# The low part of the late U blocks made by GpSimd between its row gathers instead of by VectorE

## The reference

```python
    def block(xb):
        q = (xb @ w_query).reshape(PEER_BLOCK, PEER_HEADS, 2, PEER_HALF)
        s = jnp.einsum('bhpd,phnd->bhpn', q, sub_keys).astype(jnp.float32)
        top_s, top_i = lax.top_k(s, PEER_TOPK)
        ...
        eid = e1 * PEER_NKEYS + e2
        gate = jax.nn.softmax(best_s, axis=-1)
        u_sel = expert_u[eid]
        act = jax.nn.gelu(jnp.einsum('bd,bhkd->bhk', xb, u_sel).astype(jnp.float32), approximate=False)
        v_sel = expert_v[eid]
        return jnp.einsum('bhk,bhkd->bd', (gate * act).astype(xb.dtype), v_sel)
```

## Time and profile before

| what | value |
|---|---|
| median of 3 runs | 3494.87 us (3494.62 to 3495.22) |
| profiled execution: span from the first to the last instruction | 3500.7 us |
| profiled execution: a time of its own beside the span | none is given |
| mean granted TensorE clock | 0.982 of full speed |

### The profile page before, as it was taken

One profiled execution on the slowest core, in us unless ns is written; L12 is line 12 of the kernel. 1 busy time (PEld: TensorE's weight loads), 2 busy tenths in 40 slices (PEclk: granted clock), 3 DMA queues, 4 the chain that ended last, 5 costly groups with the idle time before them and its releaser, 6 DMA issues.

```text
span 3500.7 us, 56614 instructions
## 1 busy us (share of the span) xinstructions
PE 3350.9 (96%) x21384; PEld 3291.5 (94%) x21384; DVE 2591.7 (74%) x4995; ACT 1018.7 (29%) x1349; POOL 977.2 (28%) x773
## 2 busy tenths in 40 slices
PE   6999999999998999998998899999999999999996
PEld 6999999899998999998997899999999999999996
DVE  5554444233343379999997899999999999999996
ACT  5742222321322232222543122222222222222222
POOL 0000000000000111111002555555555555555550
PEclk8999999999999999999999999999999999999998
DMA  2111011111322232334889999899998999999992
GB/s 105 40 45 36 29 36 64 68 48 42 141 85 73 89 107 102 106 112 136 266 266 307 333 337 328 318 327 326 338 329 317 327 327 340 328 321 321 329 326 104
DMA packets 304353, 698.46 MB, mean 200 GB/s; under 512 B 23873, under 2 KB 124225, under 8 KB 303201
## 3 DMA queue, kind: packets, MB, share of 16 engines
q0 software_dynamic: 98592, 362.97, 28.5%
q1 hardware_dynamic: 104112, 276.89, 23.3%
q10 hardware_dynamic: 101520, 56.89, 5.3%
HBM read 604.44 MB, written 92.22 MB: 199 GB/s over the span
## 4 chain that ended last, share of the span: by engine, by line
PE 77%; DVE 17%; DMA 2%; DVEq 2%; ACT 1%; issue 1%; ACTq 0%; SPq 0%; PEldq 0%
PE PS L1532 29%; PE PS L365 16%; PE PS L1515 14%; PE PS L1223 6%; PE PS L1253 5%; DVE HOTG L2052 3%; PE PS L1447 3%; PE PS L380 1%; DVE HOT L2048 1%; DVE HOT L2049 1%; DVE fold L1980 1%; DVE besti L1924 1%; DVE sc L1915 1%; DVE besti L1916 1%; DVEq L1978 1%
## 5 line engine op out<-in xcount | busy, mean ns | idle before, releaser
L1532 PE MATMUL PS<-AH,VH 128*128 128x368 f32 x2048 | 513.8, 332 | 20.4 <-DVE VL L2075 10.9
L1532 PE MATMUL PS<-AH,VL 128*128 128x368 f32 x2048 | 515.2, 332 | 0.0
L1532 PE MATMUL PS<-AL,VH 128*128 128x368 f32 x2048 | 509.7, 330 | 0.0
L746 POOL DMA_INDIRECT SLOT<-rows_u,EID x256 | 346.4, 1353 | 578.5 <-DVE XLF L2091 257.5
L746 POOL DMA_INDIRECT SLOT<-rows_v,EID x256 | 333.7, 1304 | 205.7 <-DVE SLOT L2082 167.5
L1532 PEld LDWEIGHTS PS<-AH,VH 128*128 128x128 f32 x2048 | 365.2, 189 | 22.7 <-DVE VL L2075 12.1
L1532 PEld LDWEIGHTS PS<-AL,VH 128*128 128x128 f32 x2048 | 366.2, 189 | 0.0
L1532 PEld LDWEIGHTS PS<-AH,VL 128*128 128x128 f32 x2048 | 365.8, 189 | 0.0
L2091 DVE SCALAR_TENSOR_TENSOR XLF<-SLOT,GA,XLF 128x1024 f32<-128x1024 f32 x256 | 328.0, 1281 | 0.5 <-DMA SLOT<-rows_v,EID 0.2
L1109 ACT ACTIVATE VH<-VRAW 128x512 fp32r<-128x512 f32 x256 | 157.8, 628 | 567.7 <-PE PS L1532 567.7
L2082 DVE SCALAR_TENSOR_TENSOR SLOT<-SLOT,XHF 128x1024 f32<-128x1024 f32 x256 | 312.6, 1221 | 3.3 <-DMA SLOT<-rows_u,EID 3.3
(11 more groups left out here) (331 smaller groups left out, 6478.3 us busy)
## 6 DMA issues: line engine op xcount, KB each, us to landing
RAW<-experts_u SPq DMA_DIRECT2D x128, 512.0 KB, 6.4
VRAW<-experts_v SPq DMA_DIRECT2D x256, 256.0 KB, 5.8
gate_matrices<-stg ACTq DMA_DIRECT2D x21, 2048.0 KB, 10.2
GW<-gate_matrices SPq DMA_DIRECT2D x96, 384.0 KB, 7.2
RAW<-weights SPq DMA_DIRECT2D x69, 512.0 KB, 3.6
activations<-AS SPq DMA_DIRECT2D x64, 368.0 KB, 2.4
AS<-activations SPq DMA_DIRECT2D x64, 368.0 KB, 3.0
GW<-gate_matrices SPq DMA_DIRECT2D x32, 320.0 KB, 6.0
```

The source lines that it names most:

```text
L746: pool.indirect_dma_start(out=SLOT[n % NSLOT][:, :], out_offset=None, in_=table, in_offset=bass.IndirectOffsetOnAxis(ap=ids, axis=0)).then ...
L1532: mm = pe.matmul(PS[:, 4 + 2 * (d % 2) + t, 0:CH], w[:, d % 2, c * P:c * P + P], x[:, c, t * CH:t * CH + CH], start=(c == 0 and n == 0), s ...
```

## The change

GpSimd's `u_low(m, slot)` computes the same subtraction as VectorE's did. It stands in the GpSimd program in each group behind the gather pair j = 2, so behind the gather for k = 5 and ahead of that for k = 6 (block m = 2g + 3), and behind the pair j = 5, so behind k = 11 and ahead of k = 12 (block m = 2g + 4). It waits for `u_hi` of its block, and for `u_lo` of the block before. VectorE's two `u_low` of each group are gone; the two of the start (`u_low(1, 0)` and `u_low(2, 1)`) stay with VectorE.

```diff
@@ gpsimd
+            def u_low(m, slot):
+
+                pool.wait_ge(u_lo, m - 1)
+                pool.wait_ge(u_hi, m)
+                pool.tensor_tensor(WL[:, slot, :], RAW[:, slot, :], WH[:, slot, :].bitcast(F32), ALU.subtract).then_inc(u_lo, 1)
+
             for g in range(NG - 1):
                 for j in range(SPR):
                     gather(SPR + 2 * SPR * g + 2 * j, v_rows, g, j)
                     gather(SPR + 2 * SPR * g + 2 * j + 1, u_rows, g + 1, j)
+                    if j == 2:
+                        u_low(2 * g + 3, 0)
+                    if j == 5:
+                        u_low(2 * g + 4, 1)
@@ vector, group_dve
                     dve.tensor_tensor(AL[:, k, :], AF[:, k, :], AH[:, k, :].bitcast(F32), ALU.subtract).then_inc(a_lo, 1)
                     if h == 0:
                         between(1)
-                    if not last:
-                        u_low(2 * g + (3 + h), h)
                     between(2 if h == 0 else SPR if first else 1)
```

## The result

The changed kernel takes 3678.84 us (median of 4 runs, 3672.48 to 3686.21) against 3495.05 us for the kernel before (median of 4 runs), a ratio of 1.0528 (95% interval 1.051 to 1.0545): 183.8 us slower. The profiled execution, the slowest of the four, took 3686.21 us with a span of 3684.5 us, 183.8 us more than the span before.

What follows compares the result with a forecast made beforehand. TensorE was taken to set the time in the steady state. 29 groups x (3.8 us pause + 1.9 us clock) + 3 us for groups 0 and 1 = 168 us more, giving 3660 us, range 3565 to 3725.

Steps and rivals of the forecast that it cites:

- No gain from the work taken off: VectorE, from group 2 on: two subtractions of 1.22 us fewer per group, beside a TensorE that never pauses, worth 0.
- The wait ahead of k = 6 and the chain behind it: GpSimd's queue waits for ScalarE's split; gather for k = 6 starts 6.7 us later, delaying k = 6 to 8, AF and AL.
- The size of the pause: TensorE at pair (0,3), waiting for AL of late block 1: 3.8 us in each group, bounds 2.4 to 5.1 us.
- The subtraction's time: GpSimd's subtraction in the chain: 2.40 us, the median of the selection stage, where the longest was 3.12 us.
- The 4.5 us that stood beside the rule: Pause at pair (0,3) if contention with VectorE made each subtraction take the trace's longest time: 3.8 + 0.7 = 4.5 us.
- The clock: TensorE's lower granted clock behind each pause at pair (0,3): 1.9 us more per group, bounds 0 and 2.9 us.
- The lower bound of 1.1 us: Clock cost read in the 5 us from 1920, behind the 4.08 us pause; 1.9 lies near the middle of 1.1 and 2.9.
- pause without the clock: Rival: gathers land in 5.0 us each, pause at pair (0,3) is 2.4 us and the clock holds: 3565 us, chance 0.24.
- The second subtraction: Gather for k = 12 lands by about 2526, VectorE wants it at about 2526.6: it just fits, counted as 0.
- Groups 0 and 1: Start of the stage, where the full chain doesn't apply: +3 us for both, between -2.3 and +5.4.
- Hidden or faster: Two rivals: gathers land in time, within 3 us of no change, chance 0.04; shorter start pauses give 3488 us, chance 0.03.
- More than one pause in a group: Rival: k = 12 or VL of d = 2 also late, or the long subtraction holds: 3730 us and above, chance 0.09.

Runs made afterwards that it cites:

- e2: Only the second subtraction of a group (behind the gather for k = 11) moved to GpSimd, from group 1 on, against the kernel before: 3495.94 us, ratio 1.0002.
- e10: Both subtractions on GpSimd from group 1 on, behind the gathers for k = 9 and k = 11, against the kernel before: 3509.50 us, ratio 1.0042.
- e4: The kernel before, subtractions left with VectorE, but GpSimd waits for the two splits ahead of the gathers for k = 6 and k = 12: 3573.77 us, ratio 1.0224.
- e5: The changed kernel with VectorE doing AF and AL of late block 1 before rows k = 6, 7 and 8, groups 1 to 31: 3545.04 us, 1.0148 of kernel before.
- e3: The changed kernel with both GpSimd subtractions moved behind the gathers for k = 9 and k = 13: 3547.29 us, ratio 1.0145 to the kernel before.
- e9: The changed kernel with GpSimd's subtraction replaced by a one-input copy of RAW to WL (wrong values): 3621.87 us, ratio 1.0345 to the kernel before.
- e1: Only the first subtraction of a group (behind the gather for k = 5) moved to GpSimd, from group 1 on, against the kernel before: 3673.20 us, ratio 1.0501.
- e6: The changed kernel with GpSimd's subtractions moved behind the gathers for k = 9 and k = 15, in all groups: 3541.79 us, ratio 1.0126 to the kernel before.
- e8: The changed kernel with the first subtraction moved one gather pair later, behind that for k = 7: 3584.94 us, ratio 1.0244 to the kernel before.

## Why the prediction was right

Forecast were 3660 us, measured 3679. The sum was 29 x 5.7 + 3 = 168 us; measured were 29 x 6.1 and about 6, 184 us. The way of the loss is shown. That the size came so near is in part luck: terms of the chain were off against each other, and a delay that I had put at 0 was hidden by the slow clock.

- **No gain from the work taken off.** Shown by e2: 1.2 us less for VectorE in each group win nothing. e10 takes 2.4 us off and has a small pause of its own, so it can only be said to agree.
- **The wait ahead of k = 6 and the chain behind it.** Shown by the chain of the changed kernel step for step, by e4 (the wait alone costs 79 us) and by e5 (the chain cut: 134 us back).
- **The size of the pause.** Forecast 3.8, measured 4.1 us in the mean, with terms off against each other. From the end of the split at 2626.0 to the issue of the gather for k = 6 it took 3.7 us; forecast were 2.7, by a subtraction of 2.40. The series of landings of the earlier trace rows, 5.0, 6.2 and 7.0 us, was not what came: in this group k = 6 took 6.0, k = 7 5.5 and k = 8 6.0. So VectorE got k = 6 2.0 us later than forecast, but then did not wait for k = 7, where I had 1.7 us of wait, nor for k = 8, where I had 0.25. AL starts 14.3 us behind the split's end, forecast 14.1. The issues of this series in the changed kernel (k = 6, 7 and 8; us to landing):

```profile
SLOT<-rows_v,EID POOLq DMA_INDIRECT x1, 6.0
SLOT<-rows_u,EID POOLq DMA_INDIRECT x1, 5.5
...
SLOT<-rows_v,EID POOLq DMA_INDIRECT x1, 6.0
```

- **The subtraction's time** is the term that was mis-sized: 2.40 us taken, 3.42 measured. I had kept the median of the selection stage because VectorE "mostly waits while the first subtraction of a group runs or directly after it". It doesn't: VectorE is in k = 4 when the subtraction starts, and goes on to AL. The rule of the Trainium skill (GPSIMD Engine Reference, 8. Key points), that VectorE's instructions with two SBUF inputs contend with GpSimd, was the better guide, and the trace agrees with it: AL, which has both inputs in SBUF, took 3.12 us beside the subtraction and 0.92 without. The 4.5 us that stood beside the rule went by the longest row, 3.12 us; even that length is exceeded.
- **The clock.** Forecast 1.9 us behind each pause, measured 2.0, of which not all is clock: e3, at a clock of 1.00, has pauses of 1.3 us, the first and last of its 29 ending at 2036.42 and 3436.79, so a period of 50.0 us, 1.5 more than 48.5. About 0.2 us thus go with any pause. The lower bound of 1.1 us was misread: its window starts 2.2 us after TensorE had resumed at 1917.78. The 4 us from 1918 alone, in the kernel before, are at 0.60, which is 1.6 us:

```profile
1918.00:1922.00 4.00, 4.00 (x16) 4.00 (x16) 3.76 (x7) 0.63 (x1) 1.68 (x1) 0.60 0.97 386
...
1934.00:1938.00 4.00, 4.00 (x24) 3.84 (x24) 3.68 (x5) 0.00 (x0) 2.12 (x2) 1.00 0.94 306
```

The second row is the one behind the pause of 3.19 us. The rival "pause without the clock" put too much trust in it: e9 lost the clock with pauses of 2.8 us in the mean.
- **The second subtraction** at 0: right for the change (e1 within 6 us of it), but by luck. In the changed kernel it holds the VL of d = 2, which takes 1.67 us and not 0.69 and ends at 2645.11. That is in time only because TensorE runs at half clock behind its pause and comes to d = 2 at 2645.91:

```profile
2643.44 1.67 DVE L2085 TENSOR_TENSOR VL<-VRAW,VH 128x512 fp32r<-128x512 f32 x1
```
```profile
2645.91 0.50 PE L1542 MATMUL PS<-AH,VH 128*128 128x368 f32 x2
```

At full clock it would have come 3.04 us behind the start of (0,3), as in the earlier trace rows, at 2644.28, and by this estimate waited 0.8 us.
- **Groups 0 and 1.** Forecast +3 with an upper bound of 5.4, measured about +6 us.
- **The rivals.** Hidden or faster: excluded by the steady pauses. More than one pause in a group: not in the changed kernel.

## What to carry to other kernels

An instruction given to another engine's queue brings its wait along, and what stands behind it there pays: look first at what its input waits for, then at what is queued behind, then at the time itself. Here the first subtraction of a group cost 178 us and the second, the same instruction six gathers later, nothing. Where TensorE sets the pace, an offload from another engine has nothing to win, and each operand's room (here 1.0 and 0.3 us) should be read before work is moved, for a pause of some us can cost half as much again in clock, as it did here. When one delay is removed, look at what it was hiding: at full clock the second subtraction would, by the estimate above, not have been free beside the first.

## What the runs showed of the hardware

- GpSimd's subtraction and copy, and VectorE's instructions with two inputs in SBUF, shut each other out for their whole length: the second one starts its work only when the first is through. Behind VectorE's k = 4, which ends at 2627.3, the subtraction takes its 2.3 us to 2629.57; behind it AL takes 0.78 us to 2630.35, though it is booked from 2627.23. With GpSimd ahead, VL took 3.44 us (e6), AF 3.12 (e5), AL 3.12; with VectorE ahead, the subtraction took 3.4 to 3.5 us. It holds for `scalar_tensor_tensor` too (3.40 us in place of 1.28 in e6), and for a GpSimd copy with one input (e9). When the two start close together, the booked starts don't tell which gets ahead: the VL of e6 is booked 0.5 us before the subtraction and was held all the same.
- VectorE's additions with one input in PSUM weren't held: the one in e2 beside the running subtraction took 0.92 us like any other:

```profile
2601.45 0.92 DVE L2174 TENSOR_TENSOR HID<-HID,PS 128x736 f32<-128x736 f32 x1 [1.16 <-PE PS L1540]
```

- Pauses of 1.9 us in the mean (e4) left the granted clock at 1.00 from 2500 to 3000 us, those of 4.1 us brought it to 0.96. In between the length of the pause doesn't settle it. e9 has pauses of 2.4 to 3.3 us there and e8, in six of its nine groups, of 2.6 to 3.3 us; the first of these rows is e9's, the second e8's:

```profile
2500.00:3000.00 500.00, 471.87 (x2688) 468.83 (x2687) 406.95 (x523) 109.57 (x159) 278.09 (x210) 0.96 0.83 299
```
```profile
2500.00:3000.00 500.00, 477.88 (x2815) 474.22 (x2814) 456.55 (x548) 113.70 (x166) 309.92 (x212) 1.00 0.87 310
```

What makes the difference is open.
